# TensorE takes each weight chunk in two passes: the high part's products over all tiles, then the low part's

## What is computed

```python
h = rms_norm(x, norm_g) * (1.0 + scale) + shift          # latent rows; the same for the context rows
qc, kvc, kr, dq, dk, dv, sq, sk, sv, z, gm = split_cols(h @ w_in)
# three attentions give y[0], y[1], y[2]
for r, y in enumerate(ys):
    zr = z[..., r * BRANCH_W:(r + 1) * BRANCH_W]
    gr = gm[..., r * D_MODEL:(r + 1) * D_MODEL]
    terms.append(jax.nn.sigmoid(gr) * ((y * jax.nn.silu(zr)) @ w_branch[r]))
x = x + gate * ((terms[0] + terms[1] + terms[2]) @ w_out)
```

## Time and profile before

| | |
|---|---|
| median of three runs | 2356.16 us |
| the profiled execution | 2355.52 us, its span 2353.7 us |
| TensorE products | 12709, busy 2328.6 us (99%) |
| VectorE, ScalarE, GpSimd busy | 61%, 53%, 12% |
| granted clock of TensorE, mean | 0.999 |

### The profile page before, as it was taken

The page is one execution under the profiler, slowest core; times in us unless marked ns, Lnnn a source line. Parts: engine busy times, 40 slices in busy tenths (PEclk is TensorE's granted clock), DMA queues, the critical chain, the costliest instruction groups (busy, mean ns, idle before and its releaser), DMA issues.

```text
span 2353.7 us, 33611 instructions
## 1 busy us (share of the span) xinstructions
PE 2328.6 (99%) x12709; PEld 1953.3 (83%) x12709; DVE 1432.1 (61%) x2345; ACT 1253.4 (53%) x2369; POOL 289.1 (12%) x394
## 2 busy tenths in 40 slices
PE   8999999999999999999999999999999999999999
PEld 6998888788887888988878878888888888888887
DVE  4565654875657435765457575756589745565565
ACT  5553255743267333755656575564466554545643
POOL 2020033510230000011631310000000000000000
PEclk9999999999999999999999999999999999999999
DMA  8503553144530422526423524565555652655654
GB/s 260 139 21 116 167 148 102 34 135 134 161 81 13 132 90 63 137 90 181 116 71 117 162 72 155 195 203 164 179 179 180 188 169 85 198 178 180 190 169 133
DMA packets 174288, 322.86 MB, mean 137 GB/s; under 512 B 15366, under 2 KB 29824, under 8 KB 173616
## 3 DMA queue, kind: packets, MB, share of 16 engines
q1 hardware_dynamic: 168368, 303.68, 41.8%
q0 software_dynamic: 5760, 17.04, 2.8%
HBM read 313.59 MB, written 3.15 MB: 135 GB/s over the span
## 4 chain that ended last, share of the span: by engine, by line
PE 91%; DVE 3%; ACT 2%; issue 1%; POOL 1%; DMA 1%; SPq 0%; DVEq 0%; ACTq 0%; POOLq 0%
PE bank L1147 17%; PE bank L1149 17%; PE bank L1148 17%; PE bank L1254 7%; PE bank L1144 4%; PE bank L1142 4%; PE bank L1143 4%; PE bank L1184 3%; PE bank L1186 3%; PE bank L1185 3%; PE bank L1440 3%; PE bank L1463 2%; PE bank L1408 1%; DVE w_low_part L2287 1%; PE bank L1594 1%
## 5 line engine op out<-in xcount | busy, mean ns | idle before, releaser
L2287 DVE TENSOR_TENSOR w_low_part<-w_raw,w_high_part 128x1024 fp32r<-128x1024 f32 (+3 forms) x544 | 645.5, 1200 | 520.4 <-ACT w_high_part L1676 516.1
L1676 ACT ACTIVATE w_high_part<-w_raw 128x1024 fp32r<-128x1024 f32 (+3 forms) x544 | 552.6, 1029 | 621.6 <-PE bank L1149 396.2
L1147 PE MATMUL bank<-w_high_part,h_high 128*128 128x512 f32 (+3 forms) x1504 | 581.1, 386 | 1.9 <-DVE w_low_part L2287 1.5
L1149 PE MATMUL bank<-w_high_part,h_low 128*128 128x512 f32 (+3 forms) x1504 | 573.7, 381 | 0.0
L1148 PE MATMUL bank<-w_low_part,h_high 128*128 128x512 f32 (+3 forms) x1504 | 573.2, 381 | 0.0
L1147 PEld LDWEIGHTS bank<-w_high_part,h_high 128*128 128x128 f32 x1504 | 283.0, 188 | 58.3 <-DVE w_low_part L2287 4.5
L1149 PEld LDWEIGHTS bank<-w_high_part,h_low 128*128 128x128 f32 x1504 | 282.8, 188 | 53.9
L1148 PEld LDWEIGHTS bank<-w_low_part,h_high 128*128 128x128 f32 x1504 | 283.2, 188 | 50.8
L2080 ACT ACTIVATE stage<-bank,neg_max 128x512 f32<-128x512 f32 (+1 forms) x240 | 146.9, 618 | 61.6 <-DVE neg_max L2826 55.5
L1184 PE MATMUL bank<-h_high,w_high_part 128*128 128x512 f32 (+1 forms) x416 | 148.7, 357 | 0.0
L1186 PE MATMUL bank<-h_high,w_low_part 128*128 128x512 f32 (+1 forms) x416 | 148.3, 356 | 0.0
(11 more groups left out here) (410 smaller groups left out, 3849.5 us busy)
## 6 DMA issues: line engine op xcount, KB each, us to landing
w_raw<-in_w_in_dram SPq DMA_DIRECT2D x160, 512.0 KB, 3.7
w_raw<-in_a_w_in_dram SPq DMA_DIRECT2D x96, 512.0 KB, 4.2
w_raw<-in_b_w_in_dram SPq DMA_DIRECT2D x80, 512.0 KB, 4.4
w_raw<-in_w_branch_dram SPq DMA_DIRECT2D x48, 512.0 KB, 4.1
w_raw<-in_w_mod_dram SPq DMA_DIRECT2D x37, 512.0 KB, 4.0
w_raw<-in_a_w_out_dram SPq DMA_DIRECT2D x32, 512.0 KB, 4.4
w_raw<-in_c_w_in_dram SPq DMA_DIRECT2D x32, 512.0 KB, 4.3
w_raw<-in_w_out_dram SPq DMA_DIRECT2D x16, 512.0 KB, 3.9
```

Source lines behind the costliest of these rows:

```text
L1147: pe.matmul(o, high, wh, start=(k == 0), stop=False)
L1149: mm = pe.matmul(o, low, wh, start=False, stop=(k == u.kt - 1))
L1676: nc.scalar.activation(WH[:, n % PART_SLOTS, 0:kt, 0:width], raw[:, 0:kt, 0:width], ACT.Copy).then_inc(*S.up("w_high", c))
L2287: v.tensor_tensor(WL[:, s, 0:kt, 0:width], raw[:, 0:kt, 0:width], WH[:, s, 0:kt, 0:width].bitcast(F32), ALU.subtract).then_inc(*S.up("w_lo ...
```

## The change

In `gemm` and `gemm_turned` a chunk is walked over twice. The wait at its start is for the high part alone. In part 0 every tile gets its two products with the weights' high part; banks are taken there. In part 1 every tile gets its product with the weights' low part, after a wait for `w_low` that is issued once per chunk (`once`). In the unit's last chunk `fills` stands after the tile's products of part 1. The products, their number and what they add up to are the same; `gemm_by_tile`, `gemm_by_side` and `keys_and_values` are left as they are.

```diff
--- before.py
+++ after.py
@@ -1124,10 +1124,10 @@
                     if u.more.get("tail") and n == 3 and u.more["r"] == 2:
                         turn_out(u.more["l"], u.more["tail"][2][-1], 1)
                     c = u.at[n]
-                    pe.wait_ge(*S.at("w_low", c))
+                    pe.wait_ge(*S.at("w_high", c))
                     slot = part_of[c] % PART_SLOTS
-                    for t in u.tiles:
-                        if n == 0:
+                    for part, t in [(part, t) for part in range(2) for t in u.tiles]:
+                        if n == 0 and part == 0:
                             open_banks[t] = take(u.more.get("pool", "wide"), (u.key, t))
                         b = open_banks[t]
                         for kk in range(kt):
@@ -1139,14 +1139,22 @@
                                 high, low = left_all(u.left, k)
                                 block = slice(P * t, P * t + P)
                                 wh, wl = WH[:, slot, kk, block], WL[:, slot, kk, block]
-                                pe.matmul(o, wh, high, start=(k == 0), stop=False)
-                                pe.matmul(o, wh, low, start=False, stop=False)
+                                if part == 0:
+                                    pe.matmul(o, wh, high, start=(k == 0), stop=False)
+                                    pe.matmul(o, wh, low, start=False, stop=False)
+                                    continue
+                                once(S.at("w_low", c))
                                 mm = pe.matmul(o, wl, high, start=False, stop=(k == u.kt - 1))
                                 continue
                             wh, wl = WH[:, slot, kk, 0:width], WL[:, slot, kk, 0:width]
-                            pe.matmul(o, high, wh, start=(k == 0), stop=False)
-                            pe.matmul(o, high, wl, start=False, stop=False)
-                            mm = pe.matmul(o, low, wh, start=False, stop=(k == u.kt - 1))
+                            if part == 0:
+                                pe.matmul(o, high, wh, start=(k == 0), stop=False)
+                                pe.matmul(o, low, wh, start=False, stop=False)
+                                continue
+                            once(S.at("w_low", c))
+                            mm = pe.matmul(o, high, wl, start=False, stop=(k == u.kt - 1))
+                        if part == 0:
+                            continue
                         if n == len(u.chunks) - 1:
                             mm.then_inc(*fills(b))
                             if t == u.tiles[-1]:
@@ -1168,10 +1176,10 @@
                     while late and late[0][0] <= n:
                         turn(*late.pop(0)[1])
                     c = u.at[n]
-                    pe.wait_ge(*S.at("w_low", c))
+                    pe.wait_ge(*S.at("w_high", c))
                     slot = part_of[c] % PART_SLOTS
-                    for b in range(last + 1):
-                        if n == 0:
+                    for part, b in [(part, b) for part in range(2) for b in range(last + 1)]:
+                        if n == 0 and part == 0:
                             open_banks[b] = take(u.more["pool"], (u.key, b))
                         o = banks[open_banks[b]][:, a:512]
                         block = slice(P * b, P * b + P)
```

## The result

The changed kernel takes 2370.89 us, the median of four runs (2370.07 to 2372.02), against 2355.94 for the kernel before beside it (2355.43 to 2356.53). The ratio is 1.0064, 95% interval 1.0052 to 1.0075: slower by 15 us. The prediction was 2370.7, slower.

The account below looks back on a forecast made before the run. TensorE, busy for 99% of the span, was taken as the bound. Terms of 16.1 us lost and 1.5 gained, net +14.6 on 2355.5, gave 2370.1; with 0.6 for the median, 2370.7 us, range 2361 to 2379.

Parts of the forecast that it names:

- five z units: Four-tile gate units (sigmoid on ScalarE, then VectorE): the next unit waits for its fourth bank, 9.5 us lost in all.
- three t units: Four-tile branch products, evicted by VectorE alone, at 596, 881 and 903 us: fourth bank late, 2.9 us lost.
- o and L1038: Unit o (0,0), then the tile-by-tile unit: later evictions delay the low part queued behind them on VectorE, 1.8 us lost.
- z, then attention: Unit z (0,0,0) before attention: the last bank TensorE waits for comes free later, 0.75 us lost.
- rotation of layer 1: The keys' rotation: block 0 is finished 4 products later, lengthening the wait behind L2374, 0.9 us lost at most.
- end of the kernel: Last tiles: tile 1's eviction waits for tile 0's, below 0.3 us, entered in the sum as 0.25.
- low-part waits: Chunk starts no longer wait for the weights' low part: 1.5 us gained, between nothing and twice that.
- the 5 us in 500 to 535: Sign that the forecast is right: this stretch, with round 1's z units, gets longer by 5 us.
- the clock at 1.00 in the bursts: Stop-and-go stretches after z and t units; the rival, chance 0.13, had the clock drop there, adding 8 to 13 us.
- The gain without a loss: Rival, faster: four-tile units' evictions keep up and only low-part waits vanish, 2353 to 2355 us; chance 0.04.
- p = 0.84 for z: VectorE's spacing between a unit's evictions; z units would need it below 0.84 us for no late fourth bank.
- Half: Rival: the old spacing holds low-part steps or waits, so evictions are really quicker; 5.2 us net loss, 2361.3 us; chance 0.13.

Follow-up runs that it names:

- the old order with the same short step: The kernel before, with the second VectorE step of layer 0's z tiles cut to one column in place of 512: 2354.63 us, ratio 0.9995.

## Why the prediction was right

*The sum.* Forecast +14.6 us, measured 15.0 by the medians and 15.2 by the spans. Term by term from the table of starts:

| term | forecast | measured |
|---|---|---|
| five z units | 9.5 | 1.59 + 2.17 + 2.96 + 1.60 + 1.58 = 9.9 |
| three t units | 2.9 | 0.43 + 1.35 + 1.35 = 3.1 |
| o and L1038 | 1.8 | 1.79 |
| z, then attention | 0.75 | 0.74 |
| rotation of layer 1 | 0.9 | 1.2 |
| end of the kernel | 0.25 | 0.24 |
| not in the sum (93, 679 to 689, 861 us) | 0 | 0.6 |
| low-part waits | −1.5 | −0.72 − 0.85 − 0.39 − 0.40 − 0.13 = −2.5 |

The term of the low part was mis-sized. The sum took the 1.5 us of the waits' table, and 0.9 of those stand at 1351.87, just ahead of the rotation's stop:

```profile
1351.87 0.38 PE L1147 MATMUL bank<-w_high_part,h_high 128*128 128x256 f32 x1 [0.89 <-DVE w_low_part L2287]
...
1357.62 0.79 PE L1408 MATMUL bank<-k_high,q_high 64*128 64x512 f32 x2 [2.62 <-DVE stage L2374]
```

They buy nothing there. In the kernel with two passes except in a unit's last chunk, TensorE comes to the stop 0.7 us earlier, and the stop is 3.4 us long in place of 2.6. The other places gave more than their idle time, because after a stop the first product is followed by the next one 0.34 us later in place of 0.23, as here in the kernel before (and after all seven of the longer stops, above 0.3 us, at the z units and L1038 of the changed kernel, 0.34 each):

```profile
1533.22 0.50 PE L1147 MATMUL bank<-w_high_part,h_high 128*128 128x512 f32 x1 [0.41 <-DVE w_low_part L2287]
1533.56 0.40 PE L1148 MATMUL bank<-w_low_part,h_high 128*128 128x512 f32 x1
```

At 1532 the place was worth 0.71 us where the forecast's own rows read 0.57, and 0.14 came just ahead of it. The losses have the same restart in them, and a four-tile unit at 93 us that was overlooked. The rotation's 1.2 us lie above the bound that the forecast gave it (0.9); with the rotations' loop as before 0.9 of them came back. Losses of 17.6 us for 16.1 and gains of 2.5 for 1.5 have nearly cancelled: the mechanism and the large terms are right, but that the total came within half a microsecond is luck.

*What would show it.* L1038 at 2 us, the 5 us in 500 to 535 (the difference goes from 2.1 to 7.2), nothing between 1070 and 1300 and the clock at 1.00 in the bursts came as said. The chain that ended last did not get more of VectorE (3% before and after), and the waits' table did not come as said: 3.4 us for L2430 where 5 to 9 were forecast, and 1.0 for L2460 where 2 to 3 were. The table counts idle time from a product's modelled end. At 507.75 to 508.67 the table's row has 0.53, start to start it is 0.92 against 0.23, so 0.69 is lost; smaller stops, such as the 0.30 us before the product at 506.99, are not in the table at all. The loss is right by starts, and more than half of it is hidden in that table.

*The rivals.* The gain without a loss (2353 to 2355) is what the two-tile units alone do, 2354.7. The point from which it decides, p = 0.84 for z, was tried: at 0.80 the z units lose 1.3 in place of 9.9 (2.1 against the old order with the same short step). "Half" did not come: in the new order VectorE's reads have the spacing that the sum took from the old one (1.78 and 1.45 in the lines above), so its step for the low part was not inside p. The clock did not fall in the bursts: TensorE stood in pieces of 0.5 us for a third of 5.3 us, at a clock of 1.00. The rule of the Trainium skill ("TensorE: Matmul & The Clock Gate", section "A second HAM failure mode: psum-queue depth-cycling"), that small idle times between groups of products make the clock swing, gave nothing here.

What stays open is why an idle stretch of 2.0 or 3.4 us lets the clock fall in one execution and not in another.

## What to carry to other kernels

Letting a chunk wait for only half of its operands gains no more than the stops that are really there, and nothing where a longer wait follows, and it moves two other moments: when each accumulator is finished, and when the next one is needed. Where a unit fills the whole pool of banks, compare "last bank free" with "last bank wanted", both counted from the unit's last product; the spacing of the evicting engine, multiplied by the tiles less one, decides. If the order is wanted for its start, keep the old one in a unit's first and last chunk, or use it where units take turns between two sets of banks; here both were no slower than the kernel before, and not measurably faster either (ratios 0.9996 and 0.9997).

## What was not expected of the hardware

A stop costs more than its idle time: the product after it is followed 0.34 us later in place of 0.23. So a bank that was late by 0.2 us by the sum cost 0.4: the first product came 0.30 us late, and the restart added 0.11. And one and the same stop is followed by the full clock in some executions and by the lower level, 1.2 GHz, in others. After 2.0 us of waiting at L1038 the next 4.0 us had a granted clock of 1.00 in the changed kernel and 0.58 in another, a mean over both levels. After the 2.6 to 3.4 us at the rotations the clock fell in ten of the eleven profiled executions and stayed at 1.00 in one, after 3.4 us. That is 1.5 us or so from run to run, as much as several of the terms above, and a reason to settle such terms from the starts in the trace and not from the medians.
